# A first norm handed to VectorE through PSUM, with a new order of products and turns in the projection phase

## The reference

```python
h = layer_norm(x, in_ln_g, in_ln_b)                 # (x - mean) * rstd * g + b, per row
proj = h @ w_in[l]                                  # 1024 -> 1792 columns: q, k, v, u
attn = swa_gqa_with_sinks(rotary(q), rotary(k), v, sinks[l])
conv = conformer_conv(u, ...)                       # a * sigmoid(gate), 31 taps, norm, swish
h = layer_norm(ALPHA * h + concat([attn, conv]) @ w_o[l], ln1_g, ln1_b)
ffn = conv_gated_mlp(h, ...)
h = layer_norm(ALPHA * h + ffn, ln2_g, ln2_b)
```

## Time and profile before

| | us |
|---|---|
| median of 3 runs | 2172.89 |
| lowest, highest | 2169.08, 2174.68 |
| the profiled execution | 2172.2 |
| its span | 2170.4 |
| TensorE busy in the span | 2013.8 (93%) |
| VectorE, ScalarE, GpSimd busy | 1208.6, 771.7, 650.2 |

### The profile page before, as it was taken

The page is one execution under the profiler, slowest core; times in us unless marked ns, Lnnn a source line. Parts: engine busy times, 40 slices in busy tenths (PEclk is TensorE's granted clock), DMA queues, the critical chain, the costliest instruction groups (busy, mean ns, idle before and its releaser), DMA issues. The chain is left out here.

```text
span 2170.4 us, 25820 instructions
## 1 busy us (share of the span) xinstructions
PE 2013.8 (93%) x9240; PEld 1655.5 (76%) x9240; DVE 1208.6 (56%) x1295; ACT 771.7 (36%) x1199; POOL 650.2 (30%) x410
## 2 busy tenths in 40 slices
PE   4899997499999499999999999999999699999998
PEld 3788885377777388888888888888888578788886
DVE  8699875577777344343434343434343544565686
ACT  4565553366666331211121112111211233232354
POOL 4587775234444101011010210120102166530000
PEclk9999998599999799999999999999999899999999
DMA  6401112533333522112111211121112444477553
GB/s 236 149 19 68 68 63 77 156 105 124 125 119 100 176 95 90 39 68 93 52 68 39 106 68 39 68 87 58 68 39 87 151 137 150 139 224 242 186 188 135
DMA packets 187215, 233.15 MB, mean 107 GB/s; under 512 B 10976, under 2 KB 130144, under 8 KB 186592
## 3 DMA queue, kind: packets, MB, share of 16 engines
q1 hardware_dynamic: 161216, 196.71, 27.5%
q10 hardware_dynamic: 25952, 35.86, 4.6%
HBM read 147.98 MB, written 84.54 MB: 107 GB/s over the span
## 5 line engine op out<-in xcount | busy, mean ns | idle before, releaser
L1513 PE MATMUL u_mm<-u_hT_hi,u_w_hi 128*128 128x512 f32 x1408 | 548.9, 390 | 15.8 <-DVE u_hT_lo L1470 15.8
L1513 PE MATMUL u_mm<-u_hT_lo,u_w_hi 128*128 128x512 f32 x1408 | 548.5, 390 | 0.0
L1513 PE MATMUL u_mm<-u_hT_hi,u_w_lo 128*128 128x512 f32 x1408 | 548.4, 390 | 0.0
L1384 ACT COPY u_z<-u_mm 128x512 f32<-128x512 f32 x176 | 103.2, 587 | 739.9 <-PE u_mm L1513 739.9
L1436 DVE TENSOR_SCALAR u_y<-u_z,u_taps,u_bias 128x2048 f32<-128x2048 f32 x43 | 57.9, 1347 | 529.9 <-ACT u_z L1384 529.9
L1513 PEld LDWEIGHTS u_mm<-u_hT_hi,u_w_hi 128*128 128x128 f32 x1408 | 264.9, 188 | 71.5 <-DVE u_hT_lo L1470 16.6
L1513 PEld LDWEIGHTS u_mm<-u_hT_hi,u_w_lo 128*128 128x128 f32 x1408 | 264.8, 188 | 55.2
L1513 PEld LDWEIGHTS u_mm<-u_hT_lo,u_w_hi 128*128 128x128 f32 x1408 | 264.9, 188 | 54.8
L1874 PE MATMUL d_y<-d_wd_hi,d_a_hi 128*128 128x512 f32 x616 | 242.7, 394 | 28.2 <-DVE d_a_lo L1756 27.3
L1874 PE MATMUL d_y<-d_wd_lo,d_a_hi 128*128 128x512 f32 x616 | 241.6, 392 | 0.0
L1874 PE MATMUL d_y<-d_wd_hi,d_a_lo 128*128 128x512 f32 x616 | 241.4, 392 | 0.0
(11 more groups left out here) (192 smaller groups left out, 2822.2 us busy)
## 6 DMA issues: line engine op xcount, KB each, us to landing
d_a_raw<-gated_scr SPq DMA_DIRECT2D x56, 704.0 KB, 5.1
u_w_raw<-w_up SPq DMA_DIRECT2D x44, 512.0 KB, 4.6
d_wd_raw<-w_down SPq DMA_DIRECT2D x88, 256.0 KB, 5.1
gated_scr<-u_s SPq DMA_DIRECT2D x41, 512.0 KB, 2.7
gated_scr<-u_y SPq DMA_DIRECT2D x20, 512.0 KB, 3.4
a_xs<-x SPq DMA_DIRECT2D x16, 512.0 KB, 4.4
m_h_in<-h_scr SPq DMA_DIRECT2D x16, 512.0 KB, 3.4
h_scr<-m_r ACTq DMA_DIRECT2D x16, 512.0 KB, 3.3
```

The source lines that it names most:

```text
L1384: nc.scalar.copy(z[:, m, bass.ds(PAD + n * BLK, BLK)], mm[m][n][:]).then_inc(z_ok, 1)
L1513: last = nc.tensor.matmul(mm[m][n][:], w[:, m, k, :], h[:, k, bass.ts(n, BLK)], start=(k == 0 and w is w_hi and h is hT_hi), stop=(k == KT ...
```

## The change

The norm of a row tile is written into a PSUM buffer of two banks, `mm01`, which is `mm[0]` and `mm[1]` joined, and VectorE's scale reads it there and writes `hs[r]`. There is one such buffer, so a norm waits until the scale of the row before it has run (`scaled_ok`), and the wait for the landed store moves from the norm to the scale. The first block's lists of ScalarE and VectorE are written out in another order, and TensorE's loop has half sweeps in front of turns.

```diff
-        mm = [ctx.enter_context(nc.psum_tensor(f"a_mm{k}", [P, BLK], F32)) for k in range(4)]
+        mm01 = ctx.enter_context(nc.psum_tensor("a_mm01", [P, D], F32))
+        mm = [mm01[:, 0:BLK], mm01[:, BLK:D]]
+        mm += [ctx.enter_context(nc.psum_tensor(f"a_mm{k}", [P, BLK], F32)) for k in range(2, 4)]
...
             def norm(n, r):
                 act.wait_ge(nmr_ok, n + 1)
-                if not (isinstance(n, int) and n == 0):
-                    act.wait_ge(h_st[r], n * 16)
-                nc.scalar.activation(hs[r], xs[:, r, :], ACT.Identity, bias=nmr[:, r:r + 1],
+                if not (isinstance(n, int) and n == 0 and r == 0):
+                    act.wait_ge(scaled_ok, RB * n + r)
+                nc.scalar.activation(mm01[:], xs[:, r, :], ACT.Identity, bias=nmr[:, r:r + 1],
                                      scale=rstd[:, r:r + 1]).then_inc(norm_ok, 1)
...
             block_root(0)
+            norm(0, 0)
+            weights_hi(1, 0)
+            norm(0, 1)
+            weights_hi(1, 1)
+            norm(0, 2)
+            norm(0, 3)
             for r in range(RB):
-                norm(0, r)
-            weights_hi(1, 0)
-            weights_hi(1, 1)
+                hi_of(0, r)
+            block_root(1)
+            for r in range(RB):
+                norm(1, r)
...
             def scale(n, r):
                 dve.wait_ge(norm_ok, RB * n + (r + 1))
-                nc.vector.tensor_tensor(hs[r], hs[r], g_bc, ALU.mult).then_inc(scaled_ok, 1)
+                if not (isinstance(n, int) and n == 0):
+                    dve.wait_ge(h_st[r], n * 16)
+                nc.vector.tensor_tensor(hs[r], mm01[:], g_bc, ALU.mult).then_inc(scaled_ok, 1)
...
             scale(0, 0)
             scale(0, 1)
-            with dve.Fori(0, NB - 1) as n:
+            stats(1, 0)
+            scale(0, 2)
+            stats(1, 1)
+            scale(0, 3)
+            lo_of(0, 0)
+            lo_of(0, 1)
+            stats(1, 2)
+            lo_of(0, 2)
+            stats(1, 3)
+            lo_of(0, 3)
+            block_stats(1)
+            scale(1, 0)
+            scale(1, 1)
+            with dve.Fori(1, NB - 1) as n:
                 block(n, False)
...
             pe.wait_ge(wlo_ok, 2)
-            with pe.Fori(1, NB) as n:
+
+            def turn(n, r):
+                pe.wait_ge(lo_ok, RB * n + (r - 1))
+                transposes(n, r)
+
+            pe.wait_ge(lo_ok, RB)
+            sweep(0, 0, 0)
+            sweep(0, 0, 1)
+            turn(1, 0)
+            sweep(0, 1, 0)
+            turn(1, 1)
+            sweep(0, 1, 1)
+            turn(1, 2)
+            turn(1, 3)
+            with pe.Fori(2, NB) as n:
                 pe.wait_ge(lo_ok, RB * n)
-                for r in range(RB):
-                    pe.wait_ge(lo_ok, RB * n + (r - 1))
-                    transposes(n, r)
-                    sweep(n - 1, r // 2, r % 2)
+                sweep(n - 1, 0, 0)
+                turn(n, 0)
+                sweep(n - 1, 0, 1)
+                turn(n, 1)
+                sweep(n - 1, 1, 0)
+                turn(n, 2)
+                turn(n, 3)
+                sweep(n - 1, 1, 1)
```

More of the change, by code:

```diff
@@ L254, in _, with block @@
             block_root(0)
-            for r in range(RB):
-                norm(0, r)
-            weights_hi(1, 0)
-            weights_hi(1, 1)
-            def block(n, first, last):
+            norm(0, 0)
[4 more added lines that the diff above has]
+            norm(0, 3)
+            for r in range(RB):
+                hi_of(0, r)
+            block_root(1)
+            for r in range(RB):
+                norm(1, r)
+            def block(n, last):
                 hi_of(n, 0)
                 hi_of(n, 1)
-                if not first:
-                    take_a(2 * n - 2, 0, n * BLK + (HALO - BLK), 2)
+                take_a(2 * n - 2, 0, n * BLK + (HALO - BLK), 2)
                 if not last:
@@ L274, in block @@
                         norm(n + 1, r)
-                if not first:
-                    take_gate(2 * n - 1, n - 1, 3)
-            block(0, True, False)
+                take_gate(2 * n - 1, n - 1, 3)
             for f in range(ROT // 2):
@@ L282, in _ @@
             with act.Fori(1, NB - 1) as n:
-                block(n, False, False)
-            block(NB - 1, False, True)
+                block(n, False)
+            block(NB - 1, True)
             take_a(2 * NB - 2, 0, (NB - 1) * BLK + HALO, 2)
```

## The result

| | before | after |
|---|---|---|
| median of 7 runs each, same chip | 2171.35 us (2169.08 to 2174.68) | 2180.01 us (2176.72 to 2183.38) |
| ratio, 95% interval | 1 | 1.0037 (1.0028 to 1.0046) |
| profiled execution: its time, span | 2172.2, 2170.4 us | 2176.7, 2174.9 us |
| last product of the projection phase starts | 363.59 us | 372.83 us |

What follows compares the result with a forecast made beforehand. Nearly tied ScalarE and VectorE chains, about 19.2 us a round, set when TensorE's last sweeps start; a fixed 272 us follows. Start +4.4 (fast clock) or +5.2 (slow), taken +4.6: 2172.2 becomes 2176.8, plus 0.7 to the median, 2177.4; range 2171 to 2182.

Steps and rivals of the forecast that it cites:

- Scale out of PSUM: VectorE's scale reading PSUM takes 1.22 us, bounds 1.21 and 3.01; GpSimd's adds beside it meet no lock.
- The rival that the lock stays: A scale from PSUM still excludes GpSimd: a row takes about 3.5 us, total 2186 us; chance 3%.
- Norm into PSUM: ScalarE's norm written to PSUM takes about 1.21 us, against 1.25 before; bounds 1.02 and 1.25.
- One buffer for four rows: Norms and scales alternate, 2.51 us a row with 0.04 us hand-overs; four norms span 8.74 us against 5.55.
- The rival of long hand-overs: Each hand-over between ScalarE and VectorE takes 0.16 us: 2.73 us a row, total 2180 us; chance 20%.
- Block 0: First block: the norm's factors come at 33.1 us against 32.73; TensorE's products begin at 31.3 instead of 39.31.
- Block 1: Norms end at 41.85 us, table load 1.28, copy of row 0 43.15 to 44.15, subtraction at 44.3 (was 42.72).
- The later rounds: First subtraction of block 2 at 66.7 us, last round from 79.6, biases of rows 2 and 3 at 90.15, 92.55.
- TensorE's waits of 1.8, 7.1, 2.7 and 4.6 us: Waits after early sweeps in blocks 1 and 2, giving back the 8 us that the first block won.
- TensorE's clock: Half rate after idle gaps; slow case: the 4.6 us gap costs 2.6 us, 1.8 hidden, adding 0.8 to the start.
- the prediction's own sign: The forecast is right if, among other signs, TensorE's last sweep starts from 96 to 97 us; wrong if before 92.
- The rival that the lock was the bound: Row exchange hides beside other work, each round shrinks by 2.7 us to 16.5, total 2165 to 2167; chance 8%.

Runs made afterwards that it cites:

- Experiment 1: Nine position and frequency DMA issues moved from ScalarE to SyncE: ratio to the kernel before 1.0018 made on the kernel after, 1.0000 made on the kernel before.
- Experiments 3 and 4: Kernel after, issues on SyncE, rows passed in halves: 1.0009; also gate a round later, old product order: 0.9991; that with norm in SBUF: 1.0001.
- half-row kernel with late gate and old order: Kernel after with issues on SyncE, rows passed in two halves, gate moved a round later, TensorE's product order as before: ratio 0.9991 to kernel before.
- half-row kernel with late gate and new order: Kernel after with issues on SyncE, rows passed in two halves, gate moved a round later, changed product order kept: ratio 1.0026 to kernel before.

## Why the prediction was nearly right

- **Scale out of PSUM, 1.22 us, no lock:** right, 1.23. The rival that the lock stays falls.
- **Norm into PSUM, 1.21 us:** right, 1.21.
- **One buffer for four rows, 2.51 us a row, hand-over 0.04:** right in blocks 2 and 3 nearly throughout (norm 0 of block 2 ends at 59.45 and its scale starts at 59.48; that ends at 60.71 and norm 1 starts at 60.74); in block 1, which is not in the loop, the hand-over from VectorE to ScalarE takes 0.1 us. Norms start 2.50 to 2.67 us apart. From norm 0 to the end of norm 3: 9.0 us in block 1 and 8.81 in block 2 (58.24 to 67.05), forecast 8.74. The rival of long hand-overs falls (it gave 2.73 a row; its own terms, 1.21 + 1.22 + 2 x 0.16, give 2.75). That its 2180 is the measured median is luck: the time came from elsewhere.
- **Block 0, factors at 33.1, first product at 31.3:** right, 32.82 and 31.09.
- **Block 1, "Table load 1.28, copy of row 0 43.15":** wrong. The copy starts at 47.81. This is the step that failed. I listed norms, table load and copy as ScalarE's list, and left out the nine issues that stand in it between norm 3 and the loop; I had asked of the moved norms what they do to the engines, not what the instructions behind them had been hidden under. Experiment 1 gives its size: 4.6 us by the stretch, 4.65 idle in the trace.
- **The later rounds:** right, each moved by that amount. First subtraction of block 2 forecast 66.7, measured 71.44 (+4.74); last round 79.6, measured 84.54 (+4.94); biases of rows 2 and 3 90.15 and 92.55, measured 94.97 and 97.31 (+4.8).
- **TensorE's waits of 1.8, 7.1, 2.7 and 4.6 us:** measured 3.64 and 1.53 in block 1, then 6.34, 0.70, 4.40 and 0.21. The second and the fourth of the forecast are the 6.34 and the 4.40. The third came out as 0.70 instead of 2.7, as the half sweep in front of it ran at the slow clock; the 3.64 came with the late copy of block 1 and was not forecast.
- **TensorE's clock:** the slow case was the true one, at both waits. The first product is 0.79 us and the window of 62 to 67 us has the granted clock at 0.50:

```profile
62.00:67.00 5.00, 4.92 (x12) 3.86 (x13) 2.43 (x2) 2.37 (x2) 2.77 (x2) 0.50 0.84 258
```

  (window, TensorE, its loads, VectorE, ScalarE, GpSimd, granted clock, DMA). But it cost less than the 0.8 us allowed for: turn 3 still waits 0.21 us for GpSimd's add, so the slow stretch lay beneath that add altogether. The forecast had 1.8 of 2.6 us beneath it.

Sum: forecast +4.4 with the clock hidden, +4.65 for the issues and +0.2 for the rest make the +9.27 measured at 101.06. By the prediction's own sign, a last sweep from 96 to 97, the size was missed; the range to 2182 held the time because it had been left wide for other reasons than the one that came true. The rival that the lock was the bound also falls: the round grew by 3.03 us where it should have shrunk by 2.7. Experiments 3 and 4 show where it is true in part: with the exchange halved and the gate out of the round, and then by 0.5 and 1.1 us a round, not 2.7.

Open is why part of the +8.7 us of the medians did not reach the span of the profiled execution (+4.5): from its first product to the end, the last phase took 445.5 us in the trace before and 441.4 in the one after. TensorE waited 1.9 us less there (7.4 against 9.3), and in the 100 us that begin 75 us after that product it made 428 products against 413, at a granted clock of 1.00 against 0.97. Why is not shown: no experiment looked at that phase.

## What to carry to other kernels

When an instruction that never waited gets a wait for each step, look at what is queued behind it on the same engine, DMA issues above all: they were hidden beside queued work, and now start when the last wait ends. An exchange through one buffer saves the lock and pays producer plus consumer for each row (here norm plus scale, 2.5 us): weigh it as a chain, and try it with the buffer split. Work put in front of a turn, on an engine with slack, pays only if the critical engine does not then wait for that turn.

## What the runs showed of the hardware

- Nine DMA issues on ScalarE's queue took 5.6 us (40.67 to 46.25; the eight of the positions 0.64 each on average, the ninth 0.44). Beside norms already queued they cost nothing; behind a norm that waits they cost 4.65 us.
- After an idle time near 3.25 us TensorE's turn of eight products took 1.09 us in the kernel before (3.26 idle) but 1.59 in the kernel before with the issues on SyncE (3.24), and 1.97 in the half-row kernel with late gate and old order (3.27); after 3.57 us in the kernel with the PSUM norm alone it took 1.26. After only 2.24 us, in the kernel after with the old product order, it took 1.71, and the products from 63.45 to 65.15 still came 0.43 us apart. In the half-row kernel with late gate and new order, two waits of the same 3.01 us were followed by products 0.23 us apart (from 66.46) and 0.43 us apart (from 85.89). Here are the turns behind 3.27 and 2.24 us:

```profile
72.96 1.97 PE L563 MATMUL a_acc<-a_ident,a_glu 128*128 128x128 f32 x8 [3.27 <-POOL a_glu L381]
61.51 1.71 PE L558 MATMUL a_acc<-a_ident,a_glu 128*128 128x128 f32 x8 [2.24 <-POOL a_glu L377]
```

  The length of the last idle time alone doesn't tell the rate that follows. After 4.40 and 6.34 us, in the kernel after, it was the slow one.
